# All gate blocks before all up blocks in each half of an expert tile, and two blocks per VectorE product

## The reference, cut to what matters

```
D_MODEL = 1024; SEQ = 1024; N_EXPERTS = 32; TOP_K = 4; D_FF = 1024
...
    xs = hf[token_of]                                  # tokens sorted by expert
    gu = lax.ragged_dot(xs, w_gate_up, sizes) + b_gate_up[e_sorted]
    gate = jnp.minimum(gu[:, :D_FF], SWIGLU_LIMIT)
    up = jnp.clip(gu[:, D_FF:], -SWIGLU_LIMIT, SWIGLU_LIMIT)
    act = (up + 1.0) * (gate * jax.nn.sigmoid(SWIGLU_ALPHA * gate))
    out = lax.ragged_dot(act, w_down, sizes) + b_down[e_sorted]
```

## Time and profile before

| | |
|---|---|
| median of 3 runs | 2415.73 us (2414.3 to 2416.65) |
| profiled execution, its own time | 2417.63 us |
| its span, first to last instruction | 2415.5 us |
| mean granted TensorE clock | 0.945 of full speed |
| busy share of PE / PEld / DVE / ACT / POOL | 92% / 83% / 37% / 18% / 22% |
| data moved | 486.27 MB, 201 GB/s over the span |

### The profile page before, as it was taken

How to read it: one execution, slowest core, us unless ns; L and a number is a source line. 1 busy time by engine, 2 the same in 40 slices (tenths; PEclk the granted TensorE clock), 3 DMA queues, 4 the chain that set the end, 5 groups by cost and what they waited for, 6 DMA issues and landing times.

```text
span 2415.5 us, 46761 instructions
## 1 busy us (share of the span) xinstructions
PE 2218.3 (92%) x16914; PEld 2006.1 (83%) x16915; DVE 887.9 (37%) x2952; ACT 422.8 (18%) x1138; POOL 526.1 (22%) x535
## 2 busy tenths in 40 slices
PE   6999988999856889999999999999999999999992
PEld 5788874455536889999999999999999999999992
DVE  0222222333333334433343434434434334344431
ACT  1212112232211111111111111111111111111110
POOL 1222220000003222233222232222332222322231
PEclk9999997999967999999999999999999999999996
DMA  7000005121105789889897889888899878998897
GB/s 252 18 9 17 0 1 183 27 53 27 44 18 188 247 255 296 267 261 289 264 298 232 279 279 280 281 262 254 271 293 290 273 234 268 298 293 286 270 297 99
DMA packets 412565, 486.27 MB, mean 201 GB/s; under 512 B 82514, under 2 KB 366034, under 8 KB 412498
## 3 DMA queue, kind: packets, MB, share of 16 engines
q1 hardware_dynamic: 380466, 441.21, 56.0%
q0 software_dynamic: 32064, 44.59, 8.6%
HBM read 454.42 MB, written 35.52 MB: 203 GB/s over the span
## 4 chain that ended last, share of the span: by engine, by line
PE 89%; issue 4%; DVE 2%; SPq 1%; ACT 1%; DMA 1%; POOL 1%; DVEq 0%; ACTq 0%; POOLq 0%
PE psum L928 22%; PE psum L944 20%; PE psum L932 20%; PE psum L753 7%; PE psum L885 5%; PE psum L917 3%; PE psum L766 1%; PE psum L836 1%; PE psum L870 1%; PE psum L835 1%; PE psum L801 1%; PE psum L769 1%; PE psum L807 1%; PE psum L853 1%; PE psum L895 1%
## 5 line engine op out<-in xcount | busy, mean ns | idle before, releaser
L928 PE MATMUL psum<-area 128*128 128x128 f32 (+2 forms) x4096 | 564.3, 294 | 4.2 <-issue 4.2
L928 PEld LDWEIGHTS psum<-area 128*128 128x128 f32 x4096 | 536.2, 201 | 6.5 <-issue 5.4
L932 PE MATMUL psum<-area 128*128 128x128 f32 (+2 forms) x4096 | 535.5, 284 | 0.0
L944 PE MATMUL psum<-area 128*128 128x128 f32 (+2 forms) x4096 | 504.4, 283 | 15.7 <-issue 15.6
L932 PEld LDWEIGHTS psum<-area 128*128 128x128 f32 x4096 | 513.4, 194 | 0.0
L944 PEld LDWEIGHTS psum<-area 128*128 128x128 f32 x4096 | 493.4, 191 | 20.8 <-issue 20.8
L1249 DVE TENSOR_SCALAR area<-psum,area 128x160 f32<-128x160 f32 x256 | 97.9, 382 | 805.6 <-PE psum L932 741.0
L529 POOL COPY area<-area 128x5 uint32 (+1 forms) x33 | 6.3, 191 | 1419.5 <-DVE area L1230 1419.5
L697 ACT ACTIVATE area<-area 128x160 f32<-128x160 f32 x256 | 85.6, 334 | 1171.9 <-DVE area L1249 911.4
L542 POOL DMA_INDIRECT sum_rows<-area x165 | 258.8, 1569 | 72.4 <-issue 58.5
L532 POOL DMA_INDIRECT area<-normed_rows,area x165 | 172.4, 1045 | 68.0 <-issue 40.2
(11 more groups left out here) (204 smaller groups left out, 1528.3 us busy)
## 6 DMA issues: line engine op xcount, KB each, us to landing
area<-in_w_gate_up SPq DMA_DIRECT2D x256, 1024.0 KB, 6.7
area<-in_w_down SPq DMA_DIRECT2D x128, 1024.0 KB
area<-in_x SPq DMA_DIRECT2D x16, 512.0 KB, 3.8
area<-in_w_in SPq DMA_DIRECT2D x1, 4096.0 KB, 13.3
area<-in_w_o SPq DMA_DIRECT2D x1, 4096.0 KB, 14.2
sum_rows<-area SPq DMA_DIRECT2D x32, 128.0 KB, 2.9
normed_rows<-area SPq DMA_DIRECT2D x8, 512.0 KB, 2.8
out<-sum_rows SPq DMA_DIRECT2D x4, 1024.0 KB, 14.0
```

Source lines behind the costliest of these rows:

```text
L928: mm(bk[:, 0:width], w_gu[2 * q][:, k, cc:cc + P], xT[:, k, 0:width], start=(k == 0), stop=(k == KD - 1))
L932: ins = mm(bk[:, SLOTS:SLOTS + width], w_gu[2 * q + 1][:, k, cc:cc + P], xT[:, k, 0:width], start=(k == 0), stop=(k == KD - 1))
L944: ins = mm(bank[2 + d // 3][:, (d % 3) * SLOTS:(d % 3) * SLOTS + width], w_dn[q][:, kk, d * P:(d + 1) * P], actT[:, 2 * q + kk, 0:width], ...
```

## The change: gate first, then up, with pieces of four contraction steps

In each half, TensorE now computes all four gate blocks, then all four up blocks. Each of these is done in two steps over the contraction: the first four steps of all four blocks, then the other four. A weight piece holds 512 columns by 4 contraction steps where it held 256 columns by 8. Gate uses PSUM banks 0 and 1, up 2 and 3, `down` 4 to 6. `refill` waits for each gate and up piece by itself.

VectorE's clamps keep their size. The two multiplications and the (up + 1) of `product` now take two blocks (320 columns) at once, and so does the sigmoid. The gate times sigmoid part has a function of its own, `gated`. In the first half the list is now: gate clamps of all four blocks, `gated` twice, then `rows_out`, `index_out` and `select`, then `product` for blocks 0 and 1 (two up clamps, (up + 1), the product), and `product` for blocks 2 and 3. `down` waits once for each q, for both its blocks. `sum_halves` makes three additions instead of eight, and a memset of PSUM ahead of the tiles is gone.

```diff
             def weights(e, h, piece, signal):
                 if piece < 4:
-                    col = h * (FF // 2) + (piece // 2) * 256 + (piece % 2) * FF
-                    src = w_gu_v[bass.ds(e, 1), :, :, col:col + 256]
+                    col = h * (FF // 2) + (piece // 2) * FF
+                    k = PART * (piece % 2)
+                    src = w_gu_v[bass.ds(e, 1), :, k:k + PART, col:col + FF // 2]
...
             def refill(e, t, h):
                 for piece in range(PIECES):
-                    if piece in (0, 2):
-                        sp.wait_ge(gu_done, t * NC + (h - 1) * NH + piece + 2)
+                    half = 2 * (h - 1)
+                    if piece == 0:
+                        sp.wait_ge(lo_done, t * 4 + half + 1)
+                    if piece == 1:
+                        sp.wait_ge(gate_done, t * 4 + half + 2)
+                    if piece == 2:
+                        sp.wait_ge(lo_done, t * 4 + half + 2)
+                    if piece == 3:
+                        sp.wait_ge(up_done, t * 4 + half + 2)
...
-            def sigmoid(t, c):
-                act.wait_ge(gu_read, t * 16 + 2 * c + 5)
-                A(sg[:, c % 2, :], g_c[:, c % 2, :], ACT.Sigmoid, scale=ALPHA).then_inc(sig_ready, 1)
+            def sigmoid(m, j):
+                act.wait_ge(gate_read, m * NH + NH + 2 * j + 2)
+                A(sg[:, 2 * j:2 * j + 2, :], g_c[:, 2 * j:2 * j + 2, :], ACT.Sigmoid, scale=ALPHA).then_inc(sig_ready, 1)
...
+            def gate_up(m, part, width):
+                read, done = (gate_read, gate_done) if part == 0 else (up_read, up_done)
+                pe.wait_ge(read, m * NH + NH)
+                for s in range(2):
+                    piece = 2 * part + s
+                    pe.wait_ge(w_exp_in[piece], m * 16 + 16)
+                    for c in range(NH):
+                        dst = bank[2 * part + c // 2][:, (c % 2) * SLOTS:(c % 2) * SLOTS + width]
+                        for k in range(PART):
+                            ins = mm(dst, w_gu[piece][:, k, c * P:(c + 1) * P], xT[:, PART * s + k, 0:width],
+                                     start=(s == 0 and k == 0 and c % 2 == 0), stop=(s == 1 and k == PART - 1),
+                                     skip_group_check=True)
+                        if s == 0 and c == NH - 1:
+                            ins.then_inc(lo_done, 1)
+                        if s == 1 and c % 2:
+                            ins.then_inc(done, 1)
...
             def down(m, q, width):
+                pe.wait_ge(act_ready, m * 2 + q + 1)
                 for kk in range(2):
-                    pe.wait_ge(act_ready, m * NH + 2 * q + kk + 1)
...
-                    for c in range(NH):
-                        gate_up(m, c, width)
+                    gate_up(m, 0, width)
+                    gate_up(m, 1, width)
...
+            def clamp_gate(t, h, e, j):
+                dve.wait_ge(gate_done, t * 4 + 2 * h + j + 1)
+                for c in (2 * j, 2 * j + 1):
+                    V.tensor_scalar(g_c[:, c, :], bank[j][:, (c % 2) * SLOTS:(c % 2 + 1) * SLOTS],
+                                    bguT[:, NH * h + c, bass.ds(e, 1)], LIMIT, ALU.add, ALU.min).then_inc(gate_read, 1)
+
+            def gated(t, h, j):
+                dve.wait_ge(gate_read, t * 8 + NH * h + NH + 2 * j + 2)
+                dve.wait_ge(sig_ready, t * 4 + 2 * h + j + 1)
+                ch.link(V.tensor_tensor(gs_t[:, 2 * j:2 * j + 2, :], g_c[:, 2 * j:2 * j + 2, :], sg[:, 2 * j:2 * j + 2, :],
+                                        ALU.mult))
+
+            def product(t, h, e, j):
+                dve.wait_ge(up_done, t * 4 + 2 * h + j + 1)
+                for c in (0, 1):
+                    V.tensor_scalar(u_c[:, c, :], bank[2 + j][:, c * SLOTS:(c + 1) * SLOTS],
+                                    bguT[:, NC + NH * h + 2 * j + c, bass.ds(e, 1)], -LIMIT,
+                                    ALU.add, ALU.max).then_inc(up_read, 1)
+                dve.wait_ge(up_read, t * 8 + NH * h + NH + 2 * j + 2)
+                ch.link(V.tensor_scalar(u2_t, u_c, LIMIT, 1.0, ALU.min, ALU.add))
+                V.tensor_tensor(actT[:, 2 * j:2 * j + 2, :], u2_t, gs_t[:, 2 * j:2 * j + 2, :], ALU.mult).then_inc(act_ready, 1)
...
-            V.memset(psum[:, 2 * 512:5 * 512], 0.0)
...
+                    for h in range(HALVES):
+                        clamp_gate(t, h, e, 0)
+                        clamp_gate(t, h, e, 1)
+                        gated(t, h, 0)
+                        gated(t, h, 1)
+                        if h == 0:
+                            rows_out(t)
+                            index_out(t + 1)
+                            select(t + 2)
+                        product(t, h, e, 0)
+                        product(t, h, e, 1)
                     xT_out(t + 1)
                     sum_halves(t)
```

More of the change, by code:

```diff
@@ L60 @@
 NH = NC // HALVES
+PART = 4
 ROUTE = 6
@@ L256, in build @@
         slots = [view(a, PIECE) for a in slot_at]
-        w_gu = [slots[s].rearrange("p (k n) -> p k n", k=KD) for s in range(4)]
+        w_gu = [slots[s].rearrange("p (k n) -> p k n", k=PART) for s in range(4)]
         w_dn = [slots[4 + s].rearrange("p (k n) -> p k n", k=2) for s in range(2)]
@@ L708, in _ @@
                     e = act.value_load(te_i[0:1, bass.ds(t, 1)], min_val=0, max_val=E - 1)
-                    for c in range(NH):
-                        sigmoid(t, c)
-                        if c == 2:
-                            flush_rows(t)
+                    sigmoid(t * 2, 0)
+                    sigmoid(t * 2, 1)
+                    flush_rows(t)
                     act.wait_ge(down_done, t * 4 + 2)
                     for d in range(KD):
-                        A(outT[:, d, :], bank[2 + d // 3][:, (d % 3) * SLOTS:(d % 3 + 1) * SLOTS], ACT.Identity,
+                        A(outT[:, d, :], bank[4 + d // 3][:, (d % 3) * SLOTS:(d % 3 + 1) * SLOTS], ACT.Identity,
                           bias=bdT[:, d, bass.ds(e, 1)]).then_inc(outT_ready, 1)
-                    for c in range(NH, NC):
-                        sigmoid(t, c)
+                    sigmoid(t * 2 + 1, 0)
+                    sigmoid(t * 2 + 1, 1)
                 with act.Else():
@@ L1268, in sum_halves @@
                 dve.wait_ge(outT_ready, t * 16 + 16)
-                for d in range(KD):
-                    V.tensor_tensor(outT[:, d, :], outT[:, d, :], bank[2 + d // 3][:, (d % 3) * SLOTS:(d % 3 + 1) * SLOTS],
-                                    ALU.add).then_inc(outT_ready, 1)
+                for b in range(3):
+                    n = min(3, KD - 3 * b)
+                    part = outT[:, 3 * b:3 * b + n, :]
+                    V.tensor_tensor(part, part, bank[4 + b][:, 0:n * SLOTS].rearrange("p (d s) -> p d s", d=n),
+                                    ALU.add).then_inc(outT_ready, n)
             ch.at(start)
-            V.memset(psum[:, 2 * 512:5 * 512], 0.0)
             select(0)
@@ L1283, in _ @@
                     e = dve.value_load(te_i[0:1, bass.ds(t, 1)], min_val=0, max_val=E - 1)
-                    clamp(t, e, 0)
-                    clamp(t, e, 1)
-                    product(t, 0)
-                    rows_out(t)
-                    index_out(t + 1)
-                    select(t + 2)
-                    for c in range(2, NH):
-                        clamp(t, e, c)
-                        product(t, c - 1)
-                    product(t, NH - 1)
-                    clamp(t, e, NH)
-                    for c in range(NH + 1, NC):
-                        clamp(t, e, c)
-                        product(t, c - 1)
-                    product(t, NC - 1)
+                    for h in range(HALVES):
[9 more added lines that the diff above has]
+                        product(t, h, e, 1)
                     xT_out(t + 1)
```

47 lines of the change are left out of this document (9 added, 38 removed).

## The result

The changed kernel takes 2509.16 us (median of 5 runs, 2499.19 to 2514.51) against 2415.17 us beside it. The ratio is 1.039, 95% interval 1.037 to 1.041: slower by 94 us. The forecast was 2536 us, range 2485 to 2572.

A forecast was written before the change was run, and what follows sets the result against it. It took TensorE (PE), 89% of the chain and nearly all in the expert stage, as the bound. 2417.6 + 73.0 + 4.4 + 44.4 - 1.3 = 2538.1, forecast 2536 us against the median, range 2485 to 2572.

The forecast's parts named there:

- The sum: Whole kernel: profiled 2417.6 us plus all terms gives 2538.1, put at 2536 us against the median of the runs.
- First half, the block of VectorE work: rows_out, index_out and select start 0.33 us later; up clamps come 8.53 us after the gate clamps instead of 8.20.
- First half, the product: down needs both blocks at once, so TensorE stands 3.40, 2.70 or 1.85 us by tile width: +73.0 us.
- Second half: The first product there is ready after the remaining up blocks end; down loses 0.22 us at 18 tiles, 0.05 at 8: +4.4 us.
- The clock: TensorE falls to the lower clock after 24 of the 32 first-half stalls, costing 1.85 us each: +44.4 us.
- the clock holds: Rival: both stalls per tile come as said, but TensorE's clock mostly stays up: 2492 us, chance 0.19.
- Longer spells: Rival: the clock falls behind every first-half stall and second-half ones too, or stays low longer: 2588 us, chance 0.07.
- Fewer instructions pay: Rival: product on two blocks makes VectorE early enough that TensorE's waits go: 2394 us, chance 0.03.
- Weights: Weight pieces starting one by one, earlier, gain nothing, since no wait for weights stood in the trace: 0.
- Memset: Removing the PSUM memset, alone on the way to the first tile, saves its time: -1.3 us.
- What would show it: Signs in the trace after: down idle 3 us in narrow first halves, 0.2 in second, mean clock below 0.945, no weight waits.

The follow-up runs named there:

- e1: Changed kernel with the one call select(t + 2) moved behind the products of all four blocks in first halves: 2404.27 us, ratio 0.9955 to the kernel before.
- e5: Changed kernel with sigmoid, gated and product on single blocks again and down waiting for each block, order of the list kept: 2515.99 us, ratio 1.043.
- e3: Changed kernel with the two halves written out and identity matmuls filling TensorE's stall ahead of down in first halves: 2643.01 us, ratio 1.096.
- wide-index kernels: Three kernels in which the 6 columns of each index matmul are repeated ten times: e9, e11 and one on e8 (2356.12 us, ratio 0.9755).
- e6: Changed kernel with identity matmuls ahead of down in both halves, inside the loop over the halves: 2536.23 us, ratio 1.051.
- e4: Changed kernel with weight pieces started as late and as paired as in the kernel before, their new shape kept: 2513.08 us, ratio 1.041.
- e8: e1 with (up + 1) and the product on single blocks and down waiting for each block; sigmoid and gated stay paired: 2388.33 us, ratio 0.9893.
- e11: Changed kernel with only the index matmuls made ten times as wide: 2494.45 us, ratio 1.0345.
- e2: Kernel before the change with select(t + 2) moved behind the fourth product of the first half: 2382.61 us, ratio 0.9893.
- e9: e2 with the index matmuls ahead of a tile made ten times as wide: 2360.63 us, ratio 0.9789.

## Why the prediction was right, and where it was off

*Direction and mechanism* were right: `down` is held in first halves by a product that stands behind rows_out, index_out and select. e1 removes it by moving one call, and e5, which undoes the pairing but keeps the order, does not.

*The sum:* of the 27 us between 2536 and 2509, 25 are the clock; gaps 3 us shorter, second halves 3 us longer and 1 us at the stalls make up the rest.

*First half, the block of VectorE work:* forecast 0.33 us later, measured 0.36 or 0.37. The three unknown durations: multiplication of 320 columns 0.49, measured 0.487 and 0.493; (up + 1) 0.31, measured 0.327; sigmoid 0.50, measured 0.470. The Trainium skill, page "VectorE: DVE Perf Modes", section on the TRN2 errata, gives the formula (N + 151)/0.96 ns, by which an estimate for the first is 0.49; the trace agrees.

*First half, the product:* forecast start of `down` at 3.40, 2.70, 1.85 us after TensorE's own end; measured 3.33, 2.64, 1.79, and 0.1 us more inside `down`, together 3.44, 2.73, 1.89. The term was +73.0 us, measured 72.4. That it is so close is in part luck: from the up clamps on it took 1.61 us and not 1.70, for the wait that I had put at 0.13 was 0.04, and the 0.1 us that goes with any `down` that really waits I had not seen. For the same reason the loss in the kernel before was 1.14 us at narrow tiles, not 1.04.

*Second half:* forecast +4.4, measured +7.0. The 0.22 us is right; the same 0.1 us comes on top at the 26 narrower tiles.

*The clock* is the term that was mis-sized: forecast +44.4 us, measured 29.5 at `down` less 10.3 at tile starts, **+19.2**. I had expected 24 slow downs and unchanged tile starts. Of the stalls of 3.4 us 11 of 18 were followed by the lower clock, of 2.7 us 5 of 8, of 1.9 us none of 6. The count 16 of 18 was carried over from gaps with index matmuls in them, which are not idle stretches, and from a single plain idle of 3.2 us. That starts got fewer I had not considered. Kernels with the long stall show 10 to 16 slow starts and those without 20 to 23 (e3, with its long gaps, and the wide-index kernels aside), so the link is there in these eight traces. Its cause is open: in e6 the clock did not fall at `down`, and starts were fewest.

*The rival "the clock holds"* (2492) and the forecast (2536) bracket the 2509 about evenly. *"Longer spells"* fell: of the downs in second halves behind their 0.3 us wait, none is slow. The Trainium skill, page "TensorE: Matmul & The Clock Gate", section "A second HAM failure mode", tells of a kernel in which short idles between groups of matmuls were enough; no trace here shows it for waits of 0.3, 1.1 or 1.9 us. *"Fewer instructions pay"* fell as such, but its point of decision was well placed: with select moved, the same paired instructions give 2404, where it had said 2394.

*Weights* at 0: right (e4, e8). *Memset* -1.3: its row is gone, the size is not measurable. *What would show it:* I named a mean clock below 0.945; the profiled execution has 0.945, the four others 0.938 to 0.941.

## What to carry to other kernels

When a block of work stands in an in-order queue between an operand's arrival and the operation that a busier engine waits for, ask how long the block is against the time that the other engine can fill; here 8.2 us stood against 7.1, and moving the part that nobody needs soon won back 105 us, more than the 94 that the restructuring had cost. The regrouping of matmuls, banks and transfers, which nobody had waited for, was worth nothing here, so make such a change only with the waits counted on both sides. Count what a stall does to the clock behind it as well as the stall, but take the odds from stalls of the same kind.

## What the runs showed of the hardware

- In the changed kernel TensorE's clock fell behind 3.4 us stalls in 11 of 18 cases and behind 1.9 us ones in none of 6, at some 1.7 us each (29.5/16 = 1.8 with the longer spells). With e4 and e11, which have the same stalls, it is 35 of 54 at 3.4 us, 16 of 24 at 2.7 us and 0 of 18 at 1.9 us. When identity matmuls filled the time, it fell behind none of 32 (e6).
- 40 matmuls of 60 columns cost 1.96 us where those of 6 columns cost 1.90, and with them slow tile starts fell from 20 to 3, some 30 us in the traces and 22 us between the medians (e2, e9). Padding light matmuls paid for itself.
- Writing out a loop of two halves on TensorE, for three widths, raised instruction transfers from 23 to 163 and cost about 134 us in gaps (e3 against the changed kernel), all of it in gaps in which such a transfer took place.
- Two VectorE multiplications of 160 columns with three semaphore waits between them start 0.53 us apart, of which 0.21 is idle (e5). With a single wait, for the end of the instruction before, the idle time is 0.03 (926.73 to 927.09 in the changed kernel). Pairs of blocks halve the number of the longer ones.
